# After the scan of an RWKV-7 layer: the sum of two rates on GpSimd, scale and offset on ScalarE, and VectorE's last operations laid over two chunks

## The reference, cut to what matters

```python
mean = jnp.mean(y, axis=-1, keepdims=True)            # per token and head of 64
var = jnp.mean(jnp.square(y - mean), axis=-1, keepdims=True)
yn = ((y - mean) * lax.rsqrt(var + RK_GN_EPS)).reshape(b, n, D_MODEL) * lnx_g + lnx_b
coef = jnp.einsum('bthn,zbthn,hn->bth', r, k_dir, r_k)  # z: the two directions
bonus = (coef[..., None] * v).reshape(b, n, D_MODEL)
gate = jax.nn.sigmoid(xg @ g1) @ g2
return ((yn + bonus) * gate) @ w_o
```

## Time and profile before

| | |
|---|---|
| Time, median of 3 runs | 3693.17 us (3686.23 to 3695.9) |
| The profiled execution, its own time | 3690.06 us |
| Its span, from first to last instruction | 3688.2 us |
| TensorE clock granted, mean | 0.911 of full speed |
| TensorE busy | 3121.6 us (85%) |
| VectorE busy | 1104.6 us (30%) |
| ScalarE busy | 557.5 us (15%) |
| GpSimd busy | 180.7 us (5%) |
| `stage_rwkv_out` in the span | about 988 to 1082 us |

### The profile page before, as it was taken

One profiled execution on the slowest core, in us unless ns is written; L12 is line 12 of the kernel. 1 busy time (PEld: TensorE's weight loads), 2 busy tenths in 40 slices (PEclk: granted clock), 3 DMA queues, 4 the chain that ended last, 5 costly groups with the idle time before them and its releaser, 6 DMA issues. The chain is left out here.

```text
span 3688.2 us, 61336 instructions
## 1 busy us (share of the span) xinstructions
PE 3121.6 (85%) x27303; PEld 2124.2 (58%) x27303; DVE 1104.6 (30%) x1828; ACT 557.5 (15%) x1029; POOL 180.7 (5%) x139
## 2 busy tenths in 40 slices
PE   3998489999887999995899999994897977877874
PEld 1454278888623444443899999882343644544442
DVE  0302388777442101336111111113104452110112
ACT  0001243333111000001001001001102431000001
POOL 0000011211100000000100000001000000100000
PEclk8999699999978999996899999996996788999997
DMA  8322311211213423713577777651301004899995
GB/s 347 133 71 79 94 50 51 66 45 43 105 52 93 119 81 108 272 65 138 188 246 254 274 266 250 225 205 52 116 23 63 1 1 205 355 427 426 426 428 195
DMA packets 246714, 612.22 MB, mean 166 GB/s; under 512 B 27188, under 2 KB 136278, under 8 KB 230968
## 3 DMA queue, kind: packets, MB, share of 16 engines
q1 hardware_dynamic: 217704, 522.93, 38.5%
q10 hardware_dynamic: 15968, 54.41, 3.8%
q0 software_dynamic: 12784, 30.99, 3.1%
HBM read 565.64 MB, written 42.63 MB: 165 GB/s over the span
## 5 line engine op out<-in xcount | busy, mean ns | idle before, releaser
L2655 PE MATMUL ps<-moe_xt,moe_wb 128*128 128x152 f32 (+1 forms) x3520 | 457.2, 292 | 2.3 <-DVE moe_xt L2817 2.3
L2655 PEld LDWEIGHTS ps<-moe_xt,moe_wb 128*128 128x128 f32 x3520 | 452.5, 194 | 2.9 <-issue 2.1
L1614 PE MATMUL ps<-ffn_h,ffn_wb 128*128 128x512 f32 x704 | 304.5, 596 | 15.5 <-PEq L1509 15.5
L2333 PE MATMUL ps<-hier_wb,hier_xt 128*64 128x256 f32 x2048 | 242.6, 393 | 75.5 <-DMA hier_wb<-in_expert_w_up 41.1
L2333 PEld LDWEIGHTS ps<-hier_wb,hier_xt 128*64 128x64 f32 x2048 | 160.7, 141 | 168.6 <-issue 66.2
L1614 PEld LDWEIGHTS ps<-ffn_h,ffn_wb 128*128 128x128 f32 x704 | 134.5, 191 | 185.6 <-issue 185.6
L2662 PE MATMUL ps<-moe_hT,moe_wb 128*128 128x152 f32 (+1 forms) x1760 | 227.2, 290 | 0.0
L2662 PEld LDWEIGHTS ps<-moe_hT,moe_wb 128*128 128x128 f32 x1760 | 222.7, 190 | 0.0
L834 PE MATMUL ps<-AT,X 64*64 64x64 f32 x4608 | 161.3, 224 | 34.2 <-DVE X L1120 18.2
L834 PEld LDWEIGHTS ps<-AT,X 64*64 64x64 f32 x4608 | 150.9, 138 | 46.7 <-issue 25.9
L1683 PE MATMUL ps<-ffn_g,ffn_wd 128*128 128x512 f32 x352 | 153.0, 598 | 2.6 <-PEq L1577 2.6
(11 more groups left out here) (479 smaller groups left out, 4020.9 us busy)
## 6 DMA issues: line engine op xcount, KB each, us to landing
moe_wb<-in_moe_w SPq DMA_DIRECT2D x60, 2048.0 KB, 10.3
hier_wb<-in_expert_w_gate SPq DMA_DIRECT2D x32, 2048.0 KB, 37.1
hier_wb<-in_expert_w_up SPq DMA_DIRECT2D x32, 2048.0 KB, 37.8
hier_wb<-in_expert_w_down SPq DMA_DIRECT2D x32, 2048.0 KB, 38.4
moe_wb<-in_moe_w SPq DMA_DIRECT2D x30, 1536.0 KB, 7.9
wb_ada<-in_ada_w SPq DMA_DIRECT2D x8, 3072.0 KB, 18.4
ada_late<-in_ada_w ACTq DMA_DIRECT2D x8, 3072.0 KB, 9.7
ffn_wb<-in_ffn_w SPq DMA_DIRECT2D x22, 1024.0 KB, 7.8
```

Source lines behind the costliest of these rows:

```text
L1614: mm = pe.matmul(k.ps[:, bank + q, :], wb[:, j, q, c, o * P:(o + 1) * P], h[:, c, :], start=c == 0, stop=c == KC - 1)
L2333: mm = pe.matmul(k.ps[both_halves(a), bank, 0:256], xs[:, c, :], wb[:, slot, at:at + 256], start=c == 0, stop=c == KC - 1)
L2655: mm = pe.matmul(k.ps[:, bank, 0:width], wb[:, slot, at:at + P], xs[:, c, :], start=c == 0, stop=c == KC - 1)
```

## The change

The addition of the two rates leaves VectorE for GpSimd, which does the eight additions after its eight products. In the second loop the scale and offset by `lnx_g` and `lnx_b` leave VectorE for ScalarE. VectorE's last two operations of a chunk become a function `gate(c)`, and VectorE's order in the second loop is now: product of chunk c by the spread `rstd`, then `gate(c - 1)`; after the loop `gate(7)`. TensorE's instructions and waits are the same.

```diff
--- before.py
+++ after.py
@@ -1268,6 +1268,11 @@
                     pool.wait_ge(k.loaded[n].sem, k.loaded[n].at(16))
                 for c in range(KC):
                     pool.tensor_tensor(r[:, c, :], r[:, c, :], kf[:, c, :], ALU.mult).then_inc(k.p_for_v.sem, 1)
+                for c in range(KC):
+                    j = c % 2
+                    pool.wait_ge(k.a_for_v.sem, k.a_for_v.at(1 + 2 * c + 1))
+                    pool.tensor_tensor(rate[:, j, 0, :], rate[:, j, 0, :], rate[:, j, 1, :], ALU.add).then_inc(
+                        k.p_for_v.sem, 1)
 
             @block.vector
             def _(dve):
@@ -1296,13 +1301,10 @@
                 def bonus_parts(c):
 
                     j = c % 2
-                    dve.wait_ge(k.a_for_v.sem, k.a_for_v.at(1 + 2 * c + 1))
-                    dve.tensor_tensor(rate[:, j, 0, :], rate[:, j, 0, :], rate[:, j, 1, :], ALU.add)
-                    dve.drain()
+                    dve.wait_ge(k.p_for_v.sem, k.p_for_v.at(KC + c + 1))
                     dve.tensor_scalar(rate[:, j, 0, :], rate[:, j, 0, :], kah[:, c:c + 1], kar[:, c:c + 1],
                                       ALU.mult, ALU.add)
                     dve.drain()
-                    dve.wait_ge(k.p_for_v.sem, k.p_for_v.at(c + 1))
                     dve.tensor_tensor(r[:, c, :], r[:, c, :], rate[:, j, 0, :], ALU.mult).then_inc(k.v_for_t.sem, 1)
 
                 bonus_parts(0)
@@ -1314,17 +1316,20 @@
                     dve.wait_ge(k.prod_v.sem, k.prod_v.at(KC + c + 1))
                     dve.tensor_tensor(kf[:, c, :], vt[:, c % 2, :], k.ps[:, c % 2, :], ALU.mult).then_inc(
                         k.v_for_a.sem, 1)
-                for c in range(KC):
-                    dve.wait_ge(k.prod_v.sem, k.prod_v.at(2 * KC + c + 1))
-                    dve.tensor_tensor(y[:, c, :], y[:, c, :], k.ps[:, 2 + c % 2, :], ALU.mult)
-                    dve.drain()
-                    dve.tensor_scalar(y[:, c, :], y[:, c, :], k.v("lnx_g")[:, c:c + 1], k.v("lnx_b")[:, c:c + 1],
-                                      ALU.mult, ALU.add)
-                    dve.drain()
+                def gate(c):
+                    dve.wait_ge(k.a_for_v.sem, k.a_for_v.at(1 + 2 * KC + c + 1))
                     dve.tensor_tensor(y[:, c, :], y[:, c, :], kf[:, c, :], ALU.add)
                     dve.drain()
                     dve.tensor_tensor(y[:, c, :], y[:, c, :], k.ps[:, 4 + c % 2, :], ALU.mult).then_inc(
                         k.v_for_t.sem, 1)
+
+                for c in range(KC):
+                    dve.wait_ge(k.prod_v.sem, k.prod_v.at(2 * KC + c + 1))
+                    dve.tensor_tensor(y[:, c, :], y[:, c, :], k.ps[:, 2 + c % 2, :], ALU.mult).then_inc(
+                        k.v_for_a.sem, 1)
+                    if c:
+                        gate(c - 1)
+                gate(KC - 1)
 
             @block.scalar
             def _(act):
@@ -1346,6 +1351,10 @@
                     act.drain().then_inc(k.a_for_v.sem, 1)
                     act.wait_ge(k.prod_a.sem, k.prod_a.at(KC + 2 * c + 2))
                     act.activation(vt[:, j, :], k.ps[:, 6 + j, :], ACT.Copy).then_inc(k.a_for_v.sem, 1)
+                for c in range(KC):
+                    act.wait_ge(k.v_for_a.sem, k.v_for_a.at(2 * KC + c + 1))
+                    act.activation(y[:, c, :], y[:, c, :], ACT.Identity, scale=k.v("lnx_g")[:, c:c + 1],
+                                   bias=k.v("lnx_b")[:, c:c + 1]).then_inc(k.a_for_v.sem, 1)
 
             @block.tensor
             def _(pe):
@@ -1403,11 +1412,11 @@
         k.loaded[n].base += 16
     k.prod_a.base += 3 * KC
     k.prod_v.base += 3 * KC
-    k.a_for_v.base += 1 + 2 * KC
+    k.a_for_v.base += 1 + 3 * KC
     k.a_for_t.base += KC
     k.v_for_t.base += 2 + 2 * KC
-    k.v_for_a.base += 2 * KC
-    k.p_for_v.base += KC
+    k.v_for_a.base += 3 * KC
+    k.p_for_v.base += 2 * KC
 
 
 def stage_project_residual(k, wb, z, gate, alpha=DN_ALPHA):
```

## The result

The changed kernel takes 3713.79 us (median of 5 runs, 3705.75 to 3722.04) against 3690.88 us before (median of 5, 3683.42 to 3695.9). The ratio is 1.0062, with a 95% interval of 1.0038 to 1.0085: it is slower by about 23 us, with 14 to 31 in the interval. The forecast was +18.5 us.

The account below looks back on a forecast made before the run. The bonus loop was taken as bound by a ScalarE-VectorE ring, the tail by TensorE at half clock. Terms 4.5 + 13.4 + 0.6 = +18.5 us on 3693.2 gave 3711.7 us, range 3702 to 3721.

Parts of the forecast that it names:

- The ring: First (bonus) loop: ScalarE and VectorE wait on each other; GpSimd's addition lengthens each chunk from 4.03 to 4.67 us.
- the sum 4.5: First loop: 0.64 us more for each of chunks 1 to 7, +4.5 us, bounds 3.6 and 5.9.
- rival C: First loop: GpSimd and VectorE meet, each chunk up to 1.26 us longer, +10 us, 3722 us; chance 5%.
- The tail's order: Second loop: TensorE waits for VectorE's delayed bank release; 6.23 us per chunk against 4.00, +13.4 us over chunks 2 to 7.
- Rival B: Second loop: TensorE is not held by the bank wait, tail stays 4.00 us per chunk, 3698 us; chance 4%.
- Scale and offset on ScalarE: Second loop: the moved 0.80 us operation runs beside TensorE's next chunk and costs nothing.
- The end: End of second loop: from VectorE's start of chunk 7, 3.45 us against 2.84 before, +0.6 us.
- The clock: TensorE's clock stays low (0.50) from the bonus loop's end through the tail, as before; no change in time.
- rival A: Second loop: TensorE's clock stays high in the tail, so not slower, -1.3 us, 3692 us; chance 6%.
- the pause of 2.90 us: Before the last head sums: TensorE idles, its clock fell about then; becoming 0.64 us longer, it speaks against a high clock.

Follow-up runs that it names:

- the best version: Kernel before plus split ScalarE wait, scale/offset on ScalarE, VectorE's two-chunk order, four PSUM bank pairs, tail's first matmul widened to 128 rows: 3672.7 us, ratio 0.9936.

## Why the prediction was right, and where a reason was wrong

The forecast held: slower by 18.5 us, measured 18.3 in the stage and 23 (14 to 31) in the whole time.

- *The ring.* Forecast 4.67 us, measured 4.61: the hand-over out of GpSimd is 0.04 instead of 0.10. That makes 7 x 0.58 = +4.1 us instead of +4.5. The tail still starts 4.4 us later against the reciprocal than before, because TensorE's first rates start 0.16 us later and the last head sums, whole at half speed now, take 0.25 more. So the sum 4.5 hit partly by luck. GpSimd's addition took 1.265 us, like its products, and did not meet VectorE: rival C did not occur.
- *The tail's order.* Forecast 6.23 us per chunk, measured 6.22, with TensorE's six waits of 2.14 us each. That is +13.3 us. Shown by letting VectorE finish each chunk (4.00) and by two more bank pairs (4.01). Rival B did not occur.
- *Scale and offset on ScalarE.* Forecast nothing; the stage was 71.1 us with it alone. `gate(7)` did not wait for it.
- *The end.* Forecast 3.45 us from VectorE's start of chunk 7; 1107.93 - 1104.51 = 3.42, +0.6 us. With this the stage is accounted for: 4.4 + 13.3 + 0.6 = 18.3.
- *The clock.* It stayed at 0.50 in the tail as forecast, so the sum stood. The step that was wrong is in the case against rival A. It rested on the pause of 2.90 us, which would become longer, and on a clock that had not risen again in 30 us. The pause does go with the moment of the fall: in both kernels the clock was down before the first narrow pass. But it did not decide the tail. With the pause filled the clock fell all the same, 3.1 us after the tail's first pass, and in the run with 128 rows it stayed high through a pause of the full 2.90 us. What keeps it low for the rest of the tail is work in that shape: every run with the 16 rows had it low to the end, and of the three with 128 rows, two never lost it there, and one won it back for 17 us. Rival A's price was right where it could be seen (a period of 4.13 us against 4.02), and its chance depended on something that I had not named. Why the chip treats the narrow passes so, no run shows, and no width between 16 and 128 rows was tried.
- *What the whole time adds.* The 23 us are 5 more than the stage. The paired traces put such differences before the stage and in the gathers, in code that did not change, and the interval takes in 18.3. Nothing more is shown.

## What to carry to other kernels

Where two engines hand work to each other through two buffers, laying one engine's operations over two chunks takes away the buffer that let them overlap: the release of chunk c - 2 must come before anything that needs chunk c - 1, or there must be more buffers (four pairs were enough here; three were not tried). An operation that moves off an engine within a ring of waits stays in the ring, at the other engine's price. Before relieving an engine, ask what bounds it: here VectorE's relief was worth nothing until TensorE's clock was up and its banks were free, and then a chunk of the tail went from 2.75 to 1.96 us.

## What the runs showed of the hardware

- The clock of TensorE followed the shape of its matmuls, not only whether it was busy. Passes over 16 and 128 rows in turn, with no gap, ran at 0.50 for more than 30 us in the kernel before (one stretch of it in the earlier trace rows), and with the pause filled they ran for 3.1 us at 1.00 before it fell to 0.50; with the 16 rows widened by zeros to 128, the clock stayed at 1.00 with TensorE busy 2.4 to 3.2 of 4 us. In the changed kernel so widened, with TensorE busy 1.9 of 4 us, it was 1.00 for 17 us and then fell. The Trainium skill (TensorE: Matmul & The Clock Gate, What's actually happening) tells of a clock that activity releases; the runs add that a TensorE that is never idle can stay on the low one.
- The narrow passes cost time at either clock as well. At 1.00 a pair of passes starts 1.05 us after the one before when 16 and 128 rows alternate, and 0.86 when all have 128; at 0.50 it is 2.00 and 1.71. The rows for this, at full clock, first with the filled pause, then the best version:

```profile
1046.78 1.12 PE L1402 MATMUL ps<-o_rstd,o_rows 16*128 16x512 f32 x2
1047.83 1.13 PE L1403 MATMUL ps<-o_hid,o_g 128*128 128x512 f32 x2
```

```profile
1055.43 1.02 PE L1414 MATMUL ps<-o_rstd,o_rows 128*128 128x512 f32 x2
...
1056.29 1.02 PE L1415 MATMUL ps<-o_hid,o_g 128*128 128x512 f32 x2
```

So the widened matmul's gain is of two kinds, and these runs do not part it further.
